# Who adds the partial sums of the experts at the end: VectorE alone, or VectorE and GpSimd

## What is computed

```
def body(acc, blk):
    tb, gb, e = blk
    xb = h[tb]
    a = jax.nn.silu(xb @ w_gate_e[e]) * (xb @ w_up_e[e])
    yb = (a @ w_down_e[e]).astype(jnp.float32)
    return acc.at[tb].add(yb * gb[:, None]), None
...
shared = (jax.nn.silu(h @ p['w_gate_s']) * (h @ p['w_up_s'])) @ p['w_down_s']
return (acc + shared.astype(jnp.float32)).astype(h.dtype)
...
x = x + ffn.reshape(bsz, length, D_MODEL).astype(x.dtype)
```

## Time and profile before

| | |
|---|---|
| median of 3 runs | 1589.52 us |
| the three runs | 1582.53, 1590.33, 1589.52 us |
| the profiled execution, its own time | 1584.53 us |
| its span, from the first to the last instruction | 1582.8 us |
| TensorE busy in the span | 1394.0 us |
| VectorE busy | 650.3 us |
| ScalarE busy | 387.5 us |
| GpSimd busy | 245.3 us |
| the tail, from the last scatter's issue to the end of the span | 1554.46 to 1582.8 us |

### The profile page before, as it was taken

One profiled execution on the slowest core, in us unless ns is written; L12 is line 12 of the kernel. 1 busy time (PEld: TensorE's weight loads), 2 busy tenths in 40 slices (PEclk: granted clock), 3 DMA queues, 4 the chain that ended last, 5 costly groups with the idle time before them and its releaser, 6 DMA issues. The chain is left out here.

```text
span 1582.8 us, 30737 instructions
## 1 busy us (share of the span) xinstructions
PE 1394.0 (88%) x10030; PEld 741.6 (47%) x10031; DVE 650.3 (41%) x1888; ACT 387.5 (24%) x1026; POOL 245.3 (15%) x287
## 2 busy tenths in 40 slices
PE   6999799999989999788878877677999989999992
PEld 3445566666667776434543322222333333444441
DVE  1423266776676766244552222121222222332333
ACT  1102255444544444320100111111111111111110
POOL 1000200005263320010000111111121211122120
PEclk9999799999999999989799988888999999999996
DMA  8312499998989999760066999999999999975835
GB/s 306 58 27 63 153 297 291 326 319 288 304 276 300 320 305 317 254 239 27 21 249 233 368 374 380 374 369 375 365 371 355 370 368 364 350 234 182 273 80 196
DMA packets 159517, 424.12 MB, mean 268 GB/s; under 512 B 47825, under 2 KB 49906, under 8 KB 133234
## 3 DMA queue, kind: packets, MB, share of 16 engines
q1 hardware_dynamic: 142912, 381.59, 66.6%
q0 software_dynamic: 14400, 38.82, 10.0%
q10 hardware_dynamic: 2098, 2.35, 0.5%
HBM read 395.25 MB, written 41.06 MB: 276 GB/s over the span
## 5 line engine op out<-in xcount | busy, mean ns | idle before, releaser
L2475 PE MATMUL ps_gu<-ring,mixT 128*32 128x512 f32 (+2 forms) x1664 | 362.4, 633 | 68.5 <-SPq L2233 67.6
L2475 PEld LDWEIGHTS ps_gu<-ring,mixT 128*32 128x32 f32 (+2 forms) x1664 | 125.0, 140 | 301.7 <-issue 251.4
L2494 PE MATMUL ps_y<-w_dn,aT_e 128*32 128x512 f32 (+2 forms) x832 | 175.9, 598 | 4.5 <-DVE aT_e L2389 1.9
L1427 PE MATMUL ps_kT<-ident,ring 128*128 128x128 f32 x1024 | 144.5, 284 | 15.9 <-DVE ring L1093 8.5
L1427 PEld LDWEIGHTS ps_kT<-ident,ring 128*128 128x128 f32 x1024 | 116.3, 146 | 75.3 <-issue 48.6
L2387 DVE TENSOR_TENSOR act_in<-sil,ps_gu 128x256 f32<-128x256 f32 x48 | 20.2, 421 | 301.8 <-ACT sil L2307 301.8
L2259 POOL DMA_INDIRECT kT<-h_dram,idx x50 | 51.9, 1037 | 587.1 <-DVE idx L2348 587.1
L2307 ACT ACTIVATE sil<-ps_gu 128x256 f32<-128x256 f32 x48 | 18.4, 383 | 408.1 <-PE ps_gu L2475 408.1
L1093 DVE COPY ring<-ps_kT 128x512 f32<-128x512 f32 x128 | 87.8, 686 | 39.4 <-PE ps_kT L1427 38.4
L2263 POOL DMA_INDIRECT sums_dram<-qT,sidx x48 | 76.5, 1593 | 147.9 <-DVE qT L2397 143.9
L2494 PEld LDWEIGHTS ps_y<-w_dn,aT_e 128*32 128x32 f32 (+2 forms) x832 | 55.4, 132 | 93.4 <-issue 85.7
(11 more groups left out here) (504 smaller groups left out, 1796.0 us busy)
## 6 DMA issues: line engine op xcount, KB each, us to landing
ring<-in_cache_k SPq DMA_DIRECT2D x256, 256.0 KB
ring<-in_cache_v SPq DMA_DIRECT2D x256, 256.0 KB, 4.6
ring<-in_w_gate_e SPq DMA_DIRECT2D x64, 1024.0 KB
ring<-in_w_up_e SPq DMA_DIRECT2D x64, 1024.0 KB
w_dn<-in_w_down_e SPq DMA_DIRECT2D x64, 1024.0 KB
w_in<-in_w_in SPq DMA_DIRECT2D x8, 1028.0 KB, 16.3
sums_dram<-w_dn SPq DMA_DIRECT2D x1, 4608.0 KB, 19.6
ring<-in_w_out SPq DMA_DIRECT2D x1, 4096.0 KB, 13.0
```

Source lines behind the costliest of these rows:

```text
L1427: last = pe.transpose(ps_kT[:, j % 2, e * PAGE:(e + 1) * PAGE], k_places[n % RING][:, e * DA + j * P:e * DA + (j + 1) * P], m.ident[:, :])
L2475: last = pe.matmul(ps_gu[at, :].rearrange("p (g n) -> p g n", g=2), xgT[:, u, k, at], w_gu[:, place, :, k, :].rearrange("p s g n -> p (s g ...
L2494: last = pe.matmul(ps_y[at, n, :], aT[:, j, at], w_dn[:, place, j, n * 512:(n + 1) * 512].rearrange("p s n -> p (s n)"), start=(j == 0), s ...
```

## The change

The adds of tiles 1 and 3 (the second and the fourth) go to GpSimd, behind its last step; VectorE keeps tiles 0, 2 and 4. Both engines use one function, `tile_sum`, which waits, adds twice with a drain between, and raises the tile's semaphore from the last add itself, with no drain behind it. `sum_done` becomes five semaphores, one for a tile, and SyncE waits for each in the same order as before.

```diff
-        sum_done, y_out = sem("sum_done"), sem("y_out")
+        sum_done, y_out = [sem(f"sum_done{t}") for t in range(TT)], sem("y_out")
+        ON_POOL = (1, 3)
+
+        def tile_sum(engine, t):
+
+            n = rows(t)
+            engine.wait_ge(sum_in[t], 16)
+            for k in range(N_SUM):
+                last = engine.tensor_tensor(m.xres[0:n, t, :], m.xres[0:n, t, :], sums[t][0:n, k * D:(k + 1) * D], ALU.add)
+                if k + 1 < N_SUM:
+                    engine.drain()
+            last.then_inc(sum_done[t], 1)
...
                 for t in range(TT):
-                    sp.wait_ge(sum_done, t + 1)
+                    sp.wait_ge(sum_done[t], 1)
                     dst = o["y_prompt"][0, t * P:(t + 1) * P, :] if t < PT else o["y_sample"].rearrange("b s d -> (b s) d")
                     sp.dma_start(dst, m.xres[0:rows(t), t, :]).then_inc(y_out, 16)
...
                 with pool.Fori(1, n_loops) as i:
                     for u in range(2):
                         step_of(i, u)
+                for t in ON_POOL:
+                    tile_sum(pool, t)
...
                 for t in range(TT):
-                    n = rows(t)
-                    dve.wait_ge(sum_in[t], 16)
-                    for k in range(N_SUM):
-                        dve.tensor_tensor(m.xres[0:n, t, :], m.xres[0:n, t, :], sums[t][0:n, k * D:(k + 1) * D], ALU.add)
-                        dve.drain()
-                    dve.sem_inc(sum_done, 1)
+                    if t not in ON_POOL:
+                        tile_sum(dve, t)
```

## The result

The changed kernel takes 1600.98 us in the median of 5 runs (1598.2 to 1605.58), the kernel before 1589.72 us (5 runs, 1582.53 to 1592.29). The ratio is 1.0085, with a 95% interval from 1.0054 to 1.0115. In a second session, side by side, 12 runs of the change had a median of 1594.93 us against 1587.59 us of 35 runs of the kernel before: ratio 1.0049, interval 1.0021 to 1.0078. By the medians the change costs 11.3 us in the first session and 7.3 in the second, where 2.7 were forecast, and the first measurement lies outside the range. (A ratio in this document is the one recorded with its interval; it differs a little from the quotient of the two medians, which is 1.0071 here.)

The account below looks back on a forecast made before the run. The tail is bound by the reads, VectorE keeping pace; removed adds are worth 0, and GpSimd's adds taking turns move the end from 1581.7 to 1584.4: 1589.52 + 2.7 = 1592.2 us, range 1583.5 to 1597.

Parts of the forecast that it names:

- What bounds the kernel: Tail after the last expert block: VectorE keeps pace with the DMA reads, so there is hardly a wait to remove.
- GpSimd's price: Tail: one dense add of 1024 columns on GpSimd estimated at 2.36 us, bounds 1.90 and 2.54.
- They take turns: Tail: GpSimd's and VectorE's adds share one queue, each handover winning 0.18 us; adds end at 1581.4 instead of 1578.7; chance 0.70.
- the forecast's sum: End of the tail: last store lands at 1584.4 instead of 1581.7 us, +2.7 us.
- the gap of 0.14 us between two dependent operations on GpSimd: Tail: time between a tile's two GpSimd adds, taken as 0.14 us from an earlier place in the trace.
- (2): Tail: four adds come back on GpSimd, a tile taking 2 x 2.36 + 0.14 = 4.9 us instead of 2.5.
- (5): Tail: removing last drains saves VectorE at most 0.05 us a tile, effectively 0; GpSimd's drains find no own DMA in flight.
- The rival on the slow side: Tail: GpSimd's first add after its indirect DMAs waits, a 10.3 us hole; +10.6 us, 1600.1 us; chance 0.05.
- slower by over 0.5%: Whole kernel: chance of a measurable slowdown, 0.05 for a hole before GpSimd's first add and 0.01 for luck of runs.

## Why the prediction was wrong

1. *What bounds the kernel* was right: the tail is the reads with VectorE at their pace, and leaving the last drains away, with five semaphores for one, changed nothing (28.2 us against 28.3 in the run with all on VectorE). What taking adds away from VectorE is worth was not measured by itself, since here they always went to GpSimd.
2. *GpSimd's price* was right: 2.34 us for an add of 1024 columns, against 2.36.
3. *They take turns* was right. GpSimd's adds in VectorE's way took 3.32 and 3.13 us, VectorE's 2.49 and 3.20 (in all 5.77 with the gap). The gain at a handover is about 0.15 us (GpSimd's add ends at 1591.14 and VectorE's, which waits for it, at 1592.21, so 1.07 us later instead of 1.22); 0.18 was assumed. The run with the early drain has a tail longer by 2.7 us, the forecast's sum; the one with the semaphore has 3.1. In the change itself the hole spread the adds, so that only two of GpSimd's lie over 2.36 us and two of VectorE's over 2.0, where at least three of each were announced.
4. **The step that failed is the gap of 0.14 us between two dependent operations on GpSimd**, in (2), and with it the sentence in (5) that GpSimd's drains find no DMA of its own in flight. The 0.14 us was read in the earlier trace rows, where no indirect DMA had gone since the last drain. In the tail the same drain stands behind 98 of them and costs 5.07 us. That all had landed does not help: I took the drain for a wait for landings, on the strength of the earlier trace rows, where it ended 0.1 to 0.3 us behind the landing. There only two DMAs lay in front of it, and at 82 ns each that is 0.16 us.
5. Of the 5.07 us, the tail got 35.3 - 31.0 = 4.3 us (3.8 in the second run of the change). The rest was used: VectorE added tile 2 in the hole without taking turns. Put on top of the forecast, 1592.2 + 4.3 = 1596.5 us would still lie inside the range, as the second session's 1594.93 does. The first session's 1600.98 us is outside by the hole and by the part ahead of the tail together, but the mechanism was wrong in either.
6. The rival on the slow side looked for a hole at the right engine and in the right kind of place, but with code for its cause, ahead of the first add. There is none ahead of it. That its 1600.1 us lies so near the first session's 1600.98 is luck. The figure of the Trainium skill, "GPSIMD Engine Reference", section on instruction dispatch, about 6 us for a freshly loaded kernel, is not this hole, and no run here shows it: the first add started 0.07 us after the landing and took its 2.34 us, and the hole comes after it and goes away with the drain. The Trainium skill, "SBUF — State Buffer", section on who interferes with whom, says that a two-input instruction of VectorE contends with a GpSimd instruction that reads SBUF and not with one that only writes it; the copies (1.86 us) and the memsets (1.23 us) beside VectorE's adds agree.
7. The chances gave 0.06 to "slower by over 0.5%". By the tail (0.40 to 0.44%) and by the second session (0.49%, 0.21 to 0.78) the change is at or just under that line; the first session is beyond it.

## What to carry to other kernels

What a drain costs is not told by the gap that another drain left elsewhere: ask what the engine has queued since its last one, and on GpSimd count the indirect DMAs. Between two dependent operations of GpSimd behind a row of indirect DMAs, wait for the first one's semaphore (two adds in 4.75 us, no hole), or put a drain where GpSimd is idle anyway (the hole was gone). And two engines that take turns at SBUF add nothing to each other: a two-input add of 1024 columns moved from VectorE to GpSimd puts 2.2 us into the shared queue and takes 1.1 out.

## What was not expected of the hardware

A `pool.drain()` on GpSimd took 82 ns for each indirect DMA of 128 rows since the last drain (1.66 us for 20, 3.62 for 44, 5.58 for 68), though all had landed; 96 and 98 cost only 4.77 and 4.93 us, and the drain of line 63, 27.7 us behind the last of 98, 0.11, which both stay unexplained. A drain also waits for a DMA in flight (42 of 46 ended 0.12 to 0.13 us behind the landing). When the two engines take turns, each handover gives back about 0.15 us.
